# Gathering some of the V expert rows in two pieces of partitions instead of one

## The reference

```python
expert = ia * PEER_N_KEYS + ib              # (token, head, 16): 128 experts of each token
gate = softmax(best_s)
def token_block(xb, eb, gb):                # 128 tokens at a time
    a = einsum('td,ted->te', xb, u_tab[eb])          # one dot product for each expert
    hidden = gb * gelu(a)
    return einsum('te,ted->td', hidden, v_tab[eb])   # weighted sum of the V rows
```

## Time and profile before

| | |
|---|---|
| median of three executions | 3082.0 us (3081.87 to 3086.39) |
| profiled execution: span from the first to the last instruction | 3083.2 us |
| its own time beside the span | not listed apart; the span lies 1.2 us above the median |
| PE (TensorE) busy | 2723.6 us, 88% |
| DVE (VectorE) busy | 2111.9 us, 68% |
| ACT (ScalarE) busy | 1146.2 us, 37% |
| POOL (GpSimd) busy | 988.0 us, 32%, nearly all of it in the expert stage |
| first gather issued, last gather issued | 1807.6 us, 3052.2 us |

### The profile page before, as it was taken

How to read it: one execution, slowest core, us unless ns; L and a number is a source line. 1 busy time by engine, 2 the same in 40 slices (tenths; PEclk the granted TensorE clock), 3 DMA queues, 4 the chain that set the end, 5 groups by cost and what they waited for, 6 DMA issues and landing times.

```text
span 3083.2 us, 34652 instructions
## 1 busy us (share of the span) xinstructions
PE 2723.6 (88%) x12212; PEld 1969.0 (64%) x12212; DVE 2111.9 (68%) x2870; ACT 1146.2 (37%) x1980; POOL 988.0 (32%) x567
## 2 busy tenths in 40 slices
PE   9999999999999999999999975666666877669997
PEld 8888788888887888999889872222223433235433
DVE  5687665555564545445566688887888887679877
ACT  5455555555553335445665530000002330034000
POOL 0021000000000000000000038777778777878864
PEclk9999999999999999999999997898999888988999
DMA  7444455555555555453354459999999999999997
GB/s 271 151 155 164 173 178 183 189 190 190 190 177 191 184 185 183 178 182 135 127 191 173 164 228 415 419 409 410 408 417 411 416 407 402 420 376 383 409 402 305
DMA packets 123586, 827.89 MB, mean 269 GB/s; under 512 B 22167, under 2 KB 22183, under 8 KB 23855
## 3 DMA queue, kind: packets, MB, share of 16 engines
q0 software_dynamic: 79392, 510.36, 40.8%
q1 hardware_dynamic: 43920, 313.73, 28.5%
q10 hardware_dynamic: 144, 2.10, 0.2%
HBM read 892.00 MB, written 4.22 MB: 291 GB/s over the span
## 4 chain that ended last, share of the span: by engine, by line
PE 58%; POOL 14%; DMA 11%; DVE 9%; issue 5%; ACT 3%; DVEq 0%; SPq 0%; ACTq 0%
PE ps L608 49%; POOL rows L1324 14%; DMA rows<-peer_u,arena 7%; PE ps L1230 2%; DMA rows<-peer_v,arena 2%; DMA rows<-peer_v 2%; DVE arena L2449 2%; PE ps L1241 2%; DVE WL L506 1%; PE ps L716 1%; ACT arena L1800 1%; DVE arena L209 1%; DVE arena L202 1%; PE ps L916 0%; DVE arena L203 0%
## 5 line engine op out<-in xcount | busy, mean ns | idle before, releaser
L506 DVE SCALAR_TENSOR_TENSOR WL<-ring,PA,WH 128x512 fp32r<-128x512 f32 x896 | 633.1, 753 | 461.7 <-ACT WH L490 445.1
L1241 PE MATMUL ps<-rows,rstd 128*128 128x512 f32 x1164 | 629.6, 694 | 300.1 <-DMA rows<-peer_v,arena 216.9
L2449 DVE CUSTOM_DVE_ANT_0 arena<-rows,arena 128x2048 f32<-128x2048 f32 x256 | 586.9, 2293 | 155.7 <-DMA rows<-peer_u,arena 128.9
L1241 PEld LDWEIGHTS ps<-rows,rstd 128*128 128x128 f32 x1164 | 245.8, 221 | 670.5 <-issue 371.9
L1324 POOL DMA_INDIRECT rows<-peer_v,arena x256 | 484.0, 1891 | 196.8 <-DVE arena L2449 73.4
L489 ACT ACTIVATE WH<-ring,PA 128x512 fp32r<-128x512 f32 x448 | 324.2, 724 | 550.1 <-PE ps L608 401.7
L1324 POOL DMA_INDIRECT rows<-peer_u,arena x256 | 451.4, 1763 | 165.7 <-DVE WL L506 85.9
L608 PE MATMUL ps<-WH,HH 128*128 128x512 f32 x1120 | 442.8, 395 | 4.0 <-DVE WL L506 4.0
L608 PE MATMUL ps<-WH,HL 128*128 128x512 f32 x1120 | 438.0, 391 | 0.0
L608 PE MATMUL ps<-WL,HH 128*128 128x512 f32 x1120 | 437.9, 391 | 0.0
L490 ACT ACTIVATE WH<-ring,PA 128x512 fp32r<-128x512 f32 x448 | 317.2, 708 | 0.0
(11 more groups left out here) (367 smaller groups left out, 3538.0 us busy)
## 6 DMA issues: line engine op xcount, KB each, us to landing
ring<-stream SPq DMA_DIRECT2D x292, 1024.0 KB, 4.8
rows<-peer_v POOLq DMA_DIRECT2D x32, 1024.0 KB, 15.4
rows<-peer_u,arena POOLq DMA_INDIRECT x256, 14.8
rows<-peer_v,arena POOLq DMA_INDIRECT x256, 15.0
arena<-xT SPq DMA_DIRECT2D x4, 512.0 KB, 9.3
bias_rows<-bias_scratch POOLq DMA_DIRECT2D x1, 2048.0 KB, 10.5
arena<-xT ACTq DMA_DIRECT2D x1, 2048.0 KB, 9.5
arena<-memT POOLq DMA_DIRECT2D x1, 2048.0 KB, 10.7
```

Of the source, the lines that this page charges most:

```text
L506: ins = nc.vector.scalar_tensor_tensor(out=half_tile(WL, u)[:, s], in0=raw_half(u)[:, s], scalar=gain[d], in1=half_tile(WH, u).bitcast(f32 ...
L1241: last = mm(ps[:, 4 * tt + q, :], DIAG[:, k % DIAGS, :], rows[:, SLOTS[n % ROWS], q * CH:(q + 1) * CH], start=n == mine[0], stop=n == ends[q])
L2449: ins = V.tensor_tensor_reduce(out=JUNK, in0=rows[:, SLOTS[n % ROWS], :], in1=HN[:, tt, :], scale=1.0, scalar=0.0, op0=ALU.mult, op1=ALU.a ...
```

## The change

Of the 256 v steps, those with j % 3 = 0 are gathered whole as before. Those with j % 3 = 1 become two gathers, partitions 0 to 63 and 64 to 127. Those with j % 3 = 2 become two gathers, 0 to 95 and 96 to 127. Both pieces go to the same slot and raise the same semaphore by 16 each, so a list `ROW_LANDED` now gives the value to wait for. The u and dense steps are as before. A gather takes its row numbers from the first partitions of a tile, so `choose` also copies those of partitions 64 to 127 and 96 to 127 to partition 0 and on, into `IDW`, which lies over parameters no longer used. The copies are posted side by side, and one wait between the writes to `IDV` and `IDU` is gone.

```diff
+PARTS = ((0, P), (0, 64, P), (0, 96, P))
+def gather_parts(n):
+    tab, g, j = ROW_ORDER[n]
+    parts = PARTS[j % len(PARTS)] if tab == "v" else PARTS[0]
+    return list(zip(parts, parts[1:]))
+ROW_LANDED = []
+for _n in range(N_ROWS):
+    ROW_LANDED.append((ROW_LANDED[_n - ROWS] if _n >= ROWS else 0) + 16 * len(gather_parts(_n)))
...
+        IDW = PA[:, W_POS:W_POS + TT * PEER_E].bitcast(u32)
...
# dense_rows, gathered_rows and dve_row alike
-                pe.wait_ge(sem(f"row_in{n % ROWS}"), 16 * (n // ROWS + 1))
+                pe.wait_ge(sem(f"row_in{n % ROWS}"), ROW_LANDED[n])
...
-                nc.gpsimd.indirect_dma_start(
-                    out=rows[:, SLOTS[n % ROWS], :], out_offset=None, in_=u_tab if tab == "u" else v_tab,
-                    in_offset=bass.IndirectOffsetOnAxis(ap=(IDU if tab == "u" else IDV)[:, at:at + 1], axis=0),
-                    bounds_check=last_row, oob_is_err=False).then_inc(sem(f"row_in{n % ROWS}"), 16)
+                for p0, p1 in gather_parts(n):
+                    ids = IDU if tab == "u" else IDW if p0 else IDV
+                    nc.gpsimd.indirect_dma_start(
+                        out=rows[p0:p1, SLOTS[n % ROWS], :], out_offset=None, in_=u_tab if tab == "u" else v_tab,
+                        in_offset=bass.IndirectOffsetOnAxis(ap=ids[0:p1 - p0, at:at + 1], axis=0),
+                        bounds_check=last_row, oob_is_err=False).then_inc(sem(f"row_in{n % ROWS}"), 16)
...
-                ch.link(V.tensor_copy(IDV[:, tt * PEER_E + 16 * h:tt * PEER_E + 16 * h + 16], SKIP))
-                ch.mark(V.tensor_copy(IDU[:, tt * PEER_E + 16 * h:tt * PEER_E + 16 * h + 16], ID), "experts_ready")
+                at = tt * PEER_E + 16 * h
+                ch.post(V.tensor_copy(IDV[:, at:at + 16], SKIP))
+                for k, (_, p0, *_) in enumerate(PARTS):
+                    if p0 < P:
+                        ch.post(V.tensor_copy(IDW[0:P - p0, at + k:at + 16:len(PARTS)], SKIP[p0:P, k:16:len(PARTS)]))
+                ch.mark(V.tensor_copy(IDU[:, at:at + 16], ID), "experts_ready")
```

More of the change, by code:

```diff
@@ L2444, in dve_row @@
                 done = ROW_DONE[n][1]
-                dve.wait_ge(sem(f"row_in{n % ROWS}"), 16 * (n // ROWS + 1))
+                dve.wait_ge(sem(f"row_in{n % ROWS}"), ROW_LANDED[n])
                 if done > 1:
```

## The result

The changed kernel takes 3794.3 us in the median of six executions (3787.15 to 3834.11), the kernel before 3084.2 us in six on the same occasions. The ratio is 1.234, with a 95% interval of 1.2304 to 1.2376. That is slower, as forecast, but by 710 us where I had forecast 256. The measured time lies 354 us above the upper end of my range.

A forecast was written before the change was run, and what follows sets the result against it. DMA transfers were taken to bound the expert stage, with POOL having only 133 us to give. 3083.2 + 256 (narrower transfers) + 1 (casts) = 3340 us of span, median 3339 us, calls not on top; range 3110 to 3440 us.

The forecast's parts named there:

- What bounds the kernel: Expert stage: DMA engines busy throughout, within 3% of the best rate; POOL has only 133 us of slot waits to give.
- The hold of POOL's gathers behind DVE: Expert stage: a gather started under a DVE row instruction waits for its end, taking 2.14 us instead of 0.99.
- (1) More calls: POOL, expert stage: 160 further gathers cost 120 us alone, but are hidden in slot waits and slower transfers.
- The bound from below: POOL's further calls: none cheaper than a plain DMA's 0.59 us, 78 us in all, fitting the slot waits: 0.
- (2) Narrower transfers: DMA into SBUF: 64 partitions share half the ways, so split steps take extra turns; 256 us, paid in full.
- (3) The casts: DVE in choose: two casts more for each of 13 groups, up to 4 us, counted as 1.
- (4) the waits: Users of a step wait for both pieces: same instruction with a larger value, 0 by itself.
- Rival B, faster: Expert stage: pieces even out unevenly loaded DMA engines, giving 3070 us; chance 0.07.
- The sign that I took for unevenness: Expert stage: landing time rose from 11.9 to 15 us although v steps move less.
- The range: Whole kernel: 3110 to 3440 us; the forecast's own range, for transfers that lose, was 3280 to 3440.
- the top of (2): Upper end for narrower transfers in the expert stage: 160 whole turns, 390 us.

The follow-up runs named there:

- e5: Kernel before with the 160 steps split by columns, two gathers of 128 partitions x 1024 floats each: 3225.6 us beside 3082.7.
- e1: Changed kernel with only the 80 steps of j % 3 = 1 split, in 64 + 64: 3518.7 us beside 3088.4 of the kernel before.
- e2: Changed kernel with only the 80 steps of j % 3 = 2 split, in 96 + 32: 3526.0 us, 438 more than the kernel before.
- e6: Changed kernel with only the 16 steps of j = 1 split, in 64 + 64: 3166.2 us beside 3082.7 of the kernel before.
- e10: e6 with the v gathers leaving nothing out: 3307.1 us, ratio 1.0727 to the kernel before.
- e9: Kernel before with the v gathers leaving nothing out, so experts below 32 are fetched twice: 3203.4 us, ratio 1.039.
- e7: Changed kernel with all 160 split steps in 64 + 64: 3848.4 us, 766 more than the kernel before.
- e3: Changed kernel with the 160 split steps as one call into partitions 0 to 63, the rest left out: 3410.9 us beside 3088.4 of the kernel before.
- e4: As e3, same row numbers and bytes, but into partitions 32 to 95: 3020.6 us beside 3088.4 of the kernel before.
- e8: As e3, but partitions 0 to 63 where j % 3 = 1 and 64 to 127 where j % 3 = 2: 3381.2 us.
- e12: As e3, but the one piece is partitions 0 to 95: 3604.3 us beside 3079.8 of the kernel before.
- e13: As e3, but the one piece is partitions 0 to 31: 3115.5 us beside 3079.8 of the kernel before.
- e11: Changed kernel with every v step gathered whole, leaving only the changed casts: 3082.3 us, ratio 0.9998 to the kernel before.

## Why the prediction was right in its kind and wrong in its size

**What bounds the kernel.** Right. The transfers had no slack, and what they lost was paid in full: q0's time rose by 688 us and the kernel's by 710. One reading was too kind: 412 GB/s is within 3% of 424, but the 402 of the last stretch is 5% below. The hold of POOL's gathers behind DVE is there too, and in e5 it is what decides.

**(1) More calls.** Right. I took 120 us for the calls if nothing else changes, and e5 has 143. The bound from below was too low: a call for fewer partitions is hardly cheaper (0.947 against 1.00 us), so 160 of them with their gaps are 200 us, over the 133 of slot waits, and 0 could not have come out. In the changed kernel these calls cost next to nothing, as I argued: they lie in 805 us of waits for a slot.

**(2) Narrower transfers.** The kind is right: DMA share near 1.0, a falling rate, longer landings and longer waits for slots, all as listed for it. The size is the step that failed: 1.83 to 2.44 us for a step of 64 + 64 and half of that for 96 + 32, 256 us in all. Measured are 5.4 us for 64 + 64 (e1) and 5.5 for 96 + 32 (e2), and 710 us in all. I had counted ways into SBUF that a piece reaches, so that 96 partitions were as good as 128, and only the halves paid, once. The runs show something else: what a step pays goes about by the number of rows that it moves in pieces laid out otherwise than a whole step, and 96 partitions are no better than 64 or 32.

| run | steps | rows a step | more, us | ns a row | more time of q0, us | ns a row |
|---|---|---|---|---|---|---|
| e1, 64 + 64 | 80 | 96 | 430 | 56 | 420 | 55 |
| e2, 96 + 32 | 80 | 96 | 438 | 57 | 448 | 58 |
| e6, 64 + 64, lone | 16 | 96 | 83.5 | 54 | 87 | 57 |
| e10 less e9, nothing left out | 16 | 128 | 103.7 | 51 | 81 | 40 |
| the changed kernel | 160 | 96 | 710 | 46 | 688 | 45 |
| e7, 64 + 64 | 160 | 96 | 766 | 50 | 773 | 50 |
| e3 less e4, one piece of 64 | 160 | 48 | 390 | 51 | 407 | 53 |

(A step moves 0.75 of 128 rows. The time of q0 is its share times the span. No price of a call is taken off: POOL waits 604 us for slots in e1 and 222 us in e6, so the further calls are hidden there.) A row in a whole step takes 2.47 us / 128 = 19 ns of the stage. With 40 to 58 ns more, a row in such a piece takes 59 to 77 ns, 3 to 4 times as long. The rule is rough: at the 56 ns of the 80-step kernels the changed kernel would be 860 us slower, and it is 710. Why crowded steps cost less each is open.

The partitions explain which pieces suffer, as far as the runs go. The Trainium skill (DMA: Bandwidth & Descriptors, The descriptor swizzle) says that in a transfer of 128 partitions every engine writes to one SBUF port of its own. The Trainium skill (the same page, Why a DMA increments its semaphore by 16 and not by 1) says that the number of engines is the largest up to 16 that divides the partitions, so 16 for 32, 64, 96 and 128 alike. If fewer partitions are dealt out in order, which no run shows and which is not how the list of the Trainium skill deals out 128, then 64 partitions from 32 on leave each engine at a port of its own, and those from 0 or 64 on do not: e4 is the cheap one, and e3, e8, e12 and e13 are the dear ones. The port table of the Trainium skill (SBUF — State Buffer, Door 1) counts only how many ports a range reaches, which would make 0 to 95 as good as 128; e12 shows that it is not.

So that engines meet at a port is argued and not shown; that the partitions written decide is shown (e3, e4). If two engines at one way cost each twice the time, that explains 1.83 of the 5.2 us of a lone split (e6). Why it is 2.9 times as much stays open. It is not drift between the engines (e10), nor uneven use of the halves over the stage (e8). The packets show where a part of it lies: some 300 are slowed by a lone split of 96 rows, so most of them belong to whole gathers beside it. What slows those is not shown.

**(3) The casts, (4) the waits.** Right. In e11's trace the first and the last of the casts start 0.60 us apart (1891.11 and 1891.71) where it was 0.21, a little over my 0.3 us more, and its time shows no change. The larger values in the waits cost nothing that e5, which has them too, would show.

**Rival B, faster.** What leaving rows out costs the rate is real but small: with nothing left out (e9) the first 900 us run at 421 GB/s against 412, as its stretch shows:

```profile
...
1835.00:2735.00 900.00, 608.35 (x1256) 257.43 (x1257) 687.55 (x1096) 109.77 (x317) 613.90 (x364) 0.82 1.01 421
```

Evening it out could give back at most 2% of the stage, 20 to 25 us, and the means chosen costs some 30 times that. The sign that I took for unevenness, landings of 15 us in place of 11.9, is none: in e9, with nothing left out, the median landing is 22.2 us. None of the runs that do all of the work is faster than the kernel before.

**The range.** It came from the bounds of (1) and (2), and the top of (2), 160 turns of 2.44 us, was no bound: I took for granted that a split step at worst occupies the engines for one more whole step. A piece can slow others as well, and the trace of before, which had no narrow gather in it, gave no ceiling.

## What to carry to other kernels

Where the transfers are the bound, keep every gather on all 128 partitions; if a step must be narrower, 64 partitions from 32 on cost next to nothing here, while partitions 0 to 31, 0 to 63 or 0 to 95, or 0 to 63 and 64 to 127 in turn, slow the whole stream. A split by columns costs a fifth of one by partitions here (143 against 710 us), and there POOL's calls become the bound. And a price for a form of transfer that the trace does not show has a floor but no ceiling, so one small run of it (16 steps of e6 tell it) comes before the edit.

## What the runs showed of the hardware that I had not expected

- A row gathered into a narrow piece (partitions from 0 or 64 on) costs the stage 40 to 58 ns more, where one of a whole gather takes 19, and a piece of 96 partitions costs the most (e12, 3604 us, at 284 GB/s). Rows of whole gathers beside it are slowed too: some 300 packets for a lone split of 96 rows (e6).
- During this the DMA share reads 0.95 or more, while the rate falls from 422 to as little as 168 GB/s (e10). The share does not tell whether the engines move data at their rate; GB/s beside it does.
- The time that a gather takes on POOL hardly depends on its partitions: 0.947 us against 1.00. It depends on DVE: 2.14 us when it starts under a DVE instruction that reads two tiles from SBUF. Two calls of all 128 partitions for each of 160 steps cost 143 us (e5), with POOL's waits for slots used up.
